# First branches of a two-block transformer kernel: index queries of used tokens only, squares added by GpSimd, rotary swaps as copies, position scores in two products

## The reference, cut to what matters

```python
proj = h @ w_in                                   # c_q 384, c_kv 256, k_pe 64, gate 1024
q = (rms_norm(c_q, q_norm) @ w_uq).reshape(B, L, 8, 192)
q_nope, q_pe = q[..., :128], q[..., 128:]
kv = (rms_norm(c_kv, kv_norm) @ w_ukv).reshape(B, L, 8, 256)
q_pe, k_pe = apply_rope(q_pe, cos, sin), apply_rope(k_pe, cos, sin)   # [x1 cos - x2 sin, x1 sin + x2 cos]
s = q_nope . k_nope + q_pe . k_pe                 # per head; k_pe is shared by the heads
p = softmax(s * 192 ** -0.5);  o = p @ v          # out: (o * silu(gate)) @ w_out
...
# selective attention of the second block, per block of 128 queries
rel = relu(einsum('bqhd,bsd->bqhs', iq, ik) * 64 ** -0.5)
score = einsum('bqh,bqhs->bqs', iw * 8 ** -0.5, rel)      # then causal mask, top 128 of 512 keys
```

## Time and profile before

| | |
|---|---|
| runs | 2126.0 us median of 3 (2125.6 to 2129.88) |
| profiled execution, span | 2125.8 us |
| DVE busy | 1621.4 us, 76% |
| ACT busy | 976.6 us, 46% |
| POOL busy | 399.3 us, 19% |

### The profile page before, as it was taken

The page is one execution under the profiler, slowest core; times in us unless marked ns, Lnnn a source line. Parts: engine busy times, 40 slices in busy tenths (PEclk is TensorE's granted clock), DMA queues, the critical chain, the costliest instruction groups (busy, mean ns, idle before and its releaser), DMA issues.

```text
span 2125.8 us, 29059 instructions
## 1 busy us (share of the span) xinstructions
PE 2098.3 (99%) x10935; PEld 1832.3 (86%) x10935; DVE 1621.4 (76%) x2984; ACT 976.6 (46%) x1710; POOL 399.3 (19%) x296
## 2 busy tenths in 40 slices
PE   8999999999999999999999999999999999999998
PEld 6777788887877788789999999999998888888886
DVE  4777566664985535799999988777668888888887
ACT  5344444444234423533366657766533433333333
POOL 2000110000000001000232323222223344444440
PEclk9999999999999999999999999999999999999999
DMA  6411144531321122123788988898999999999993
GB/s 253 161 38 54 46 148 173 184 130 69 109 92 57 40 99 99 63 97 117 263 281 278 328 285 302 295 311 289 347 366 365 374 372 372 376 376 377 375 364 145
DMA packets 137436, 471.50 MB, mean 222 GB/s; under 512 B 10113, under 2 KB 59521, under 8 KB 111569
## 3 DMA queue, kind: packets, MB, share of 16 engines
q1 hardware_dynamic: 50512, 309.39, 39.9%
q0 software_dynamic: 36864, 134.23, 16.3%
q10 hardware_dynamic: 49920, 26.01, 4.2%
HBM read 417.04 MB, written 52.43 MB: 221 GB/s over the span
## 4 chain that ended last, share of the span: by engine, by line
PE 86%; DVE 10%; DMA 1%; issue 1%; ACT 1%; SPq 0%; DVEq 0%; ACTq 0%
PE bank L156 84%; DVE whl L309 2%; DMA L<-in_w_ada 1%; PE bank L668 1%; DVE L L1480 1%; DVE L L1478 1%; DVE room L2191 1%; DVE L L948 0%; DVE room L2187 0%; PE bank L1569 0%; DVE wk L1914 0%; DMA XT<-in_xT 0%; DVE L L573 0%; DVE L L1461 0%; DVE row L2247 0%
## 5 line engine op out<-in xcount | busy, mean ns | idle before, releaser
L156 PE MATMUL bank<-xhl,whl 128*128 128x384 f32 (+1 forms) x5256 | 1076.2, 361 | 12.2 <-DVE whl L519 7.9
L156 PEld LDWEIGHTS bank<-xhl,whl 128*128 128x128 f32 x5256 | 935.8, 188 | 102.4 <-ACT xhl L459 9.0
L309 DVE TENSOR_TENSOR whl<-raw,whl 128x1024 fp32r<-128x1024 f32 (+2 forms) x389 | 467.4, 1210 | 215.5 <-ACT whl L302 176.9
L156 PE MATMUL bank<-whl,ag 128*128 128x512 f32 x2304 | 526.3, 390 | 0.7 <-issue 0.7
L156 PEld LDWEIGHTS bank<-whl,ag 128*128 128x128 f32 x2304 | 431.4, 188 | 91.3 <-ACT whl L302 1.9
L302 ACT ACTIVATE whl<-raw 128x1024 fp32r<-128x1024 f32 (+2 forms) x389 | 394.3, 1032 | 86.1 <-PE bank L156 78.1
L2234 POOL DMA_INDIRECT row<-in_U_rows,row_at x128 | 177.1, 1384 | 599.2 <-DVE row L2247 431.6
L2234 POOL DMA_INDIRECT row<-in_V_rows,row_at x128 | 180.8, 1413 | 260.2 <-DVE y_tok L2263 231.0
L2263 DVE SCALAR_TENSOR_TENSOR y_tok<-row,row_a,y_tok 128x1024 f32<-128x1024 f32 x127 | 162.4, 1279 | 2.6
L2247 DVE SCALAR_TENSOR_TENSOR row<-row,h_tok 128x1024 f32<-128x1024 f32 x128 | 155.6, 1217 | 1.1 <-DMA row<-in_U_rows,row_at 1.1
L156 PE MATMUL bank<-yhl,whl 128*128 128x512 f32 x588 | 140.2, 395 | 2.7 <-DVE whl L309 2.7
(11 more groups left out here) (278 smaller groups left out, 1977.6 us busy)
## 6 DMA issues: line engine op xcount, KB each, us to landing
raw<-in_U SPq DMA_DIRECT2D x64, 1024.0 KB, 6.8
raw<-in_V SPq DMA_DIRECT2D x64, 1024.0 KB, 7.4
hidden<-h_both SPq DMA_DIRECT2D x32, 768.0 KB, 9.8
gates<-g_stage ACTq DMA_DIRECT2D x12, 2048.0 KB, 19.7
g_ring<-gates SPq DMA_DIRECT2D x32, 768.0 KB, 10.8
h_ring<-hidden SPq DMA_DIRECT2D x22, 768.0 KB, 8.4
raw<-in_w_ada SPq DMA_DIRECT2D x16, 1024.0 KB, 6.4
raw<-in_w_gla SPq DMA_DIRECT2D x12, 1024.0 KB, 4.9
```

Source lines behind the costliest of these rows:

```text
L156: return e.matmul(o, a, b, start=start, stop=stop, skip_group_check=True)
L309: e.tensor_tensor(lo[:, s], src[:, s], F(hi[:, s]), ALU.subtract).then_inc(dve_lo.of((i, half)))
```

## The change

- **Index queries** (`tensor_sel`, `scalar_sel`): only tokens 128 to 511 are projected and copied, 384 columns instead of 512.
- **Squares**: ACT's squares of the latents go to buffers of their own, GpSimd adds those of `c_q` and those of `c_kv` (three `tensor_tensor`), and PE does two `square_sums` after chunk 9 instead of five. Roots and reciprocals (ACT, DVE) move from chunk 9 to chunk 10.
- **Rotary swaps**: `swapped` copies 32 rows at a time from PSUM to the rows of the other half, four copies by ACT, in place of a matmul with `swap`, in `tensor_l0` and for each even head. ACT's copy of `qp` waits in addition until `og` of two heads before is done, since the swapped rows go to `rtmp`.
- **Position scores**: `KD` holds the high part of the keys on rows 0 to 63 and the low part on rows 64 to 127. `QD[j]` holds head j's high queries on both halves (four 64-row copies by ACT for a pair of heads), `q_low` the low parts of both heads (two 64-row subtractions by DVE). A tile takes two matmuls, `QD[j]` with `KD` and `q_low` with `KZ[j]`, instead of three.
- `consts` is laid out without `swap`, and only half of `kz` is zeroed. These lines are left out below.

```diff
         rel, reset = C("rel"), C("reset")
-        rope, swap = cst[:, 384:1408], C("swap")
+        rope = cst[:, 384:1408]
...
         CQ, CK = Parts(yhl, 2560), Parts(yhl, 2560, 3)
-        KZ = Parts(kz, 1024)
+        KZ = [kz[:, j * T:(j + 1) * T] for j in range(2)]
+        KD = kz[:, 2 * T:3 * T]
...
         l0_sq = [l0_tmp[:, 0:T], l0_tmp[:, T:2 * T]]
-        R, l0_dg2, l0_pet = l0_dg, l0_tmp[:, 2 * T:4 * T], l0_sum
+        R, l0_turn, l0_pet = l0_dg, l0_tmp[:, 2 * T:3 * T], l0_sum
+        c_square = [l0_sq[0], l0_sq[1], l0_sq[1], l0_tmp[:, 3 * T:4 * T], l0_sq[1]]
+        c_sum = [c_square[0], c_square[3]]
...
+        def swapped(e, dst, src, done, *step):
...
+            for n in range(4):
+                o = 32 * (n ^ 1)
+                copy(e, dst[32 * n:32 * n + 32], src[o:o + 32]).then_inc(done.of((*step, n)))
...
                 spent[i, ch % 2] = pe_l0, ("in", ch)
-                l0_banks.give(("in", ch), (act_l0, "pe") if ch == 5 else (dve_l0, ("leave", ch)))
+                l0_banks.give(("in", ch), (act_l0, ("swap", 3)) if ch == 5 else (dve_l0, ("leave", ch)))
...
                     l0_banks.give("x root", (act_l0, "R"))
-                for j in (0, 1) if ch == 5 else (ch - 4,) if 6 <= ch < 9 else ():
-                    b = l0_banks.fill(q, "c sum") if j == 0 else l0_banks.of["c sum"]
-                    q.wait_ge(act_l0["c square", j])
-                    square_sums(e, q, b, j // 3, l0_sq[j % 2], j == 0).then_inc(pe_l0.of(("c sum", j)))
-                    if j == 4:
-                        l0_banks.give("c sum", (act_l0, ("c root", 1)))
-                if ch == 6:
-                    b = l0_banks.fill(q, "swap")
-                    q.wait_ge(act_l0["pe"])
-                    mul(e, b, swap, l0_pet, True, True).then_inc(pe_l0.of("swap"))
-                    l0_banks.give("swap", (dve_l0, "swap"))
+                if ch == 9:
+                    b = l0_banks.fill(q, "c sum")
+                    for g in range(2):
+                        q.wait_ge(pool_l0["c sum", 2 + 2 * g])
+                        m = square_sums(e, q, b, g, c_sum[g], g == 0)
+                    m.then_inc(pe_l0.of("c sum"))
+                    l0_banks.give("c sum", (act_l0, ("c root", 1)))
...
                 for j in (0, 1) if ch == 4 else (ch - 3,) if 5 <= ch < 8 else ():
-                    q.wait_ge(dve_l0["leave", j], pe_l0["c sum", j - 2] if j >= 2 else pe_l0["x sum"])
-                    e.activation(l0_sq[j % 2], latent(j), ACT.Square).then_inc(act_l0.of(("c square", j)))
+                    q.wait_ge(dve_l0["leave", j], pe_l0["x sum"])
+                    if j in (2, 4):
+                        q.wait_ge(pool_l0["c sum", 1 if j == 2 else 2])
+                    e.activation(c_square[j], latent(j), ACT.Square).then_inc(act_l0.of(("c square", j)))
...
                     copy(e, l0_pet, l0_banks.of["in", 5]).then_inc(act_l0.of("pe"))
+                    swapped(e, l0_turn, l0_banks.of["in", 5], act_l0, "swap")
                 if ch == 7:
+                    q.wait_ge(dve_l0["kpe"], pool_l0["zeros"])
...
                         rows = slice(64 * n, 64 * n + 64)
-                        q.wait_ge(dve_l0["kpe"], pool_l0["zeros"])
-                        copy(e, KZ(n)[0][rows], kpe[rows]).then_inc(act_l0.of(("kpe", n)))
-                if ch == 9:
-                    q.wait_ge(pe_l0["c sum", 4])
+                        copy(e, KZ[n][rows], kpe[rows]).then_inc(act_l0.of(("kpe", n)))
+                    copy(e, KD[0:64], kpe[0:64]).then_inc(act_l0.of(("kpe", 2)))
+                if ch == 10:
+                    q.wait_ge(pe_l0["c sum"])
...
                 if ch == 6:
-                    q.wait_ge(pe_l0["swap"])
-                    e.tensor_tensor(l0_dg2[:, 0:T], l0_banks.of["swap"], sinT, ALU.mult).then_inc(dve_l0.of("swap"))
+                    q.wait_ge(act_l0["swap", 3])
+                    e.tensor_tensor(l0_turn, l0_turn, sinT, ALU.mult).then_inc(dve_l0.of("swap"))
                     q.wait_ge(dve_l0["swap"])
-                    e.tensor_tensor(kpe, kpe, l0_dg2[:, 0:T], ALU.add).then_inc(dve_l0.of("k turned"))
+                    e.tensor_tensor(kpe, kpe, l0_turn, ALU.add).then_inc(dve_l0.of("k turned"))
...
                 if ch == 7:
-                    for j in range(2):
-                        rows = slice(64 * j, 64 * j + 64)
-                        hi, lo = KZ(j)
-                        q.wait_ge(act_l0["kpe", j], dve_l0["kpe"], pool_l0["zeros"])
-                        e.tensor_tensor(lo[rows], kpe[rows], F(hi[rows]), ALU.subtract).then_inc(dve_l0.of(("kpe", j)))
-                if ch == 9:
+                    q.wait_ge(act_l0["kpe", 1], dve_l0["kpe"])
+                    e.tensor_tensor(KD[64:128], kpe[64:128], F(KZ[1][64:128]), ALU.subtract).then_inc(dve_l0.of("kpe low"))
+                if ch == 10:
...
         def pool_l0_sums(e, q):
-            e.memset(F(kz[:, :]), 0.0).then_inc(pool_l0.of("zeros"))
+            e.memset(F(kz[:, 0:2 * T]), 0.0).then_inc(pool_l0.of("zeros"))
...
                 e.tensor_tensor(l0_sum, l0_sum, l0_sq[(k - 1) % 2], ALU.add).then_inc(pool_l0.of(("sum", k)))
+            for j, g in ((1, 0), (2, 0), (4, 1)):
+                q.wait_ge(act_l0["c square", j])
+                if j == 2:
+                    q.wait_ge(pool_l0["c sum", 1])
+                e.tensor_tensor(c_sum[g], c_sum[g], c_square[j], ALU.add).then_inc(pool_l0.of(("c sum", j)))
...
         loc = Local(L)
-        QN, KN, QP = Parts(yhl, 512, 10), Parts(yhl, 512, 12), Parts(yhl, 512, 14)
+        QN, KN = Parts(yhl, 512, 10), Parts(yhl, 512, 12)
+        QD, q_low = [yhl[:, 14 * T:15 * T], kz[:, 3 * T:4 * T]], yhl[:, 15 * T:16 * T]
...
                     project(e, q, b, iq, 2, CQ, c_ready, 3, 384).then_inc(pe_mla.of(("qp", hd)))
-                    mla_banks.give(("qp", hd), (act_mla, ("qp", hd)))
+                    mla_banks.give(("qp", hd), (act_mla, ("swap", hd, 3)))
...
                 mla_banks.give(("q", hd), (dve_mla, ("q", hd)))
-                if j == 0:
-                    b = mla_banks.fill(q, ("swap", hd))
-                    q.wait_ge(act_mla["qp", hd])
-                    mul(e, b, swap, qraw, True, True).then_inc(pe_mla.of(("swap", hd)))
-                    mla_banks.give(("swap", hd), (dve_mla, ("sin", hd)))
-                else:
+                if j == 1:
...
                 j = hd % 2
-                q.wait_ge(dve_mla["q", hd], dve_mla["k", hd], act_mla["q turned", hd - j], dve_mla["qp", hd - j])
+                q.wait_ge(dve_mla["q", hd], dve_mla["k", hd], act_mla["q turned", hd - j, 3], dve_mla["qp", hd - j, 1])
...
                     mul3(e, b, QN(0, qt * P, (qt + 1) * P), KN(0), True)
-                    mul3(e, b, QP(0, qt * P, (qt + 1) * P), KZ(j), False, True).then_inc(pe_mla.of(("s", hd, qt)))
+                    mul(e, b, QD[j][:, qt * P:(qt + 1) * P], KD, False)
+                    mul(e, b, q_low[:, qt * P:(qt + 1) * P], KZ[j], False, True).then_inc(pe_mla.of(("s", hd, qt)))
...
                     if hd >= 2:
-                        q.wait_ge(pe_mla["swap", hd - 2], dve_mla["cos", hd - 2])
+                        q.wait_ge(dve_mla["cos", hd - 2], act_mla["og", hd - 2], dve_mla["og", hd - 2])
                     copy(e, qraw, mla_banks.of["qp", hd]).then_inc(act_mla.of(("qp", hd)))
+                    swapped(e, rtmp, mla_banks.of["qp", hd], act_mla, "swap", hd)
...
                     q.wait_ge(dve_mla["q turned", hd])
-                    copy(e, QP(0)[0], qp).then_inc(act_mla.of(("q turned", hd)))
+                    for n in range(4):
+                        rows, own = slice(64 * (n % 2), 64 * (n % 2) + 64), slice(64 * (n // 2), 64 * (n // 2) + 64)
+                        copy(e, QD[n // 2][rows], qp[own]).then_inc(act_mla.of(("q turned", hd, n)))
...
                     hi, lo = at(0)
-                    q.wait_ge(act_mla[what, hd], pe_mla[what, hd] if what in "qk" else dve_mla[what, hd])
+                    q.wait_ge(act_mla[what, hd], pe_mla[what, hd])
...
                         q.wait_ge(pe_mla["s", hd - 1, 3])
-                    e.tensor_tensor(lo, whole, F(hi), ALU.subtract).then_inc(dve_mla.of((what if what in "qk" else "qp", hd)))
+                    e.tensor_tensor(lo, whole, F(hi), ALU.subtract).then_inc(dve_mla.of((what, hd)))
...
                     if hd >= 2:
-                        q.wait_ge(act_mla["q turned", hd - 2], dve_mla["qp", hd - 2])
+                        q.wait_ge(act_mla["q turned", hd - 2, 3], dve_mla["qp", hd - 2, 1])
...
                 if hd % 2 == 0:
-                    q.wait_ge(pe_mla["swap", hd])
-                    if hd >= 2:
-                        q.wait_ge(act_mla["og", hd - 2], dve_mla["og", hd - 2])
-                    e.tensor_tensor(rtmp, mla_banks.of["swap", hd], sinT, ALU.mult).then_inc(dve_mla.of(("sin", hd)))
+                    q.wait_ge(act_mla["swap", hd, 3])
```

(31 more changed lines are left out.)

## The result

The changed kernel takes 2128.8 us (median of 20 runs, 2126.86 to 2133.85), the kernel before 2125.94 (20 runs, 2123.52 to 2130.9). The ratio is 1.0014, 95% interval 1.0008 to 1.0021: 2.9 us slower, less than the 4.3 us that the prediction counts as a change. The profiled execution has a span of 2125.4 us and a time of 2127.11. It is the third quickest of the 20, so its span does not show the 2.9 us; its stages show where time is lost and won.

The account below looks back on a forecast made before the run. Bound: the loop of DVE and `w_ada` loads in the first projections, PE in attention and before the index scores. +1.4 + 1.6 + 3.4 - 4.4 = +2.0 on 2125.8, with the median's 0.2, gave 2128.0 us; range 2119 to 2132.5.

Parts of the forecast that it names:

- First projections, saving worth 0: First projection stage: PE's saved square sums and swap, some 3.5 us, shorten nothing, as DVE and `w_ada` loads set the pace.
- The place: First projections, the spread at PE's chunk 11 that needs the reciprocal: PE idles about 3 us there, near 82 to 85.
- GpSimd's sums, +1.4: First projections: three new GpSimd sums delay DVE by 0 to 0.9 us each, taken as 0.45: +1.4 us (0 to 2.7).
- Attention's path, +1.6: Attention, even heads: the longer path through ACT and DVE makes the two-head loop 34.3 us against 33.9: +1.6 us.
- The clock, +3.4: Attention: gaps of 3.1 us before even scores drop PE to 1.2 GHz, 1.7 us per fall: +3.4 us (0 to 6.8).
- Two of four: Attention: of four chances for a clock fall ahead of even heads' scores, two were taken, halfway between two profile rows.
- Index queries, -4.4: Before the index scores: 96 products of 384 instead of 512 columns save 0.046 us each, moving later stages forward: -4.4 us.
- the overlap of copies: Rival, attention: narrow copies overlap, the clock holds, GpSimd finds free moments: -6.6 and the median's 0.2, 2119.4 us; chance 0.20.
- the saving kept by PE: Rival, attention: the new path stays hidden and PE keeps its saving of 10.8 us: -13.8, 2112.2 us; chance 0.08.
- the index stage without effect: Rival, index stage: DVE's selection is the bound, so the change has no effect there: +4.4 on the forecast, 2132.4; chance 0.06.
- No fall at all: Rival, attention: the clock never falls in the gaps before even scores: 3.4 us less, 2124.6; chance 0.18.
- Four falls in every run: Rival, attention: the clock falls before all even heads' scores, 6.8 us in place of 3.4: 2131.4; chance 0.18.

Follow-up runs that it names:

- the filled gaps: The changed kernel with useless products in TensorE's gaps ahead of the even heads' scores (13 in head 0, 9 in heads 2, 4, 6): 2125.01 us.

## Why the prediction was right

The forecast of 2128.0 lies 0.8 us below the measured median. Its terms, each against its runs (index -5.7, first projections +3.5, attention +4.9, in sum +2.7 of the 2.9 measured; each is the difference of one run to the next in a chain, so the sum is no check of them). The mechanisms held, but part of the closeness is luck: the index queries gained 1.3 us more than forecast by medians, the first projections cost 2.1 more, and the two errors largely cancel (0.4 and 1.0 by means).

- **First projections, saving worth 0:** held. The place was right in part: in four of the seven profiles with GpSimd's sums PE idles 1.1 to 1.5 us at the spread, never 3. In the changed kernel the saving is used up sooner, in waits of 0.96, 1.43 and 0.17 us from 58 to 74 us that DVE's late splits cause, and a fall of the clock behind them (0.82 in the first window above, 0.75 in the next); at the spread in the changed kernel there is no gap left.
- **GpSimd's sums, +1.4:** the mechanism held and the profiles agree in size, 0.8 to 1.3. The working behind it did not. They cost DVE 2.4 us, not half of 2.7: all three met a DVE instruction, two of them for most of a sum's length. That delay passes on in full to the next load of the loop. By the means of the same 13 profiles the load of `w_ada` near 76 us is issued 2.4 us later, and 1.0 comes back because it then lands sooner, 4.6 to 5.1 us after its issue in all seven profiles with the sums, against 6.0 to 6.7 in four of the six without and 4.7 in the other two. Why the load took longer in those four no run shows; that the net cost lies near the forecast is luck. By median times the stage costs 3.5, by means 2.4 with an interval down to 0.8, so this term may be too small; what the rest is made of no run shows.
- **Attention's path, +1.6:** held. The loop was put at 34.3 us and is 34.4; the gaps at 3.1 and are 2.15 to 3.73; narrow copies are held, at 0.61 and 0.65 us where 0.63 and 0.66 were taken. With the falls taken out, attention costs 4.9 - 3.8 = 1.1 by medians (1.4 by means).
- **The clock, +3.4:** held; 3.8 by the filled gaps. Two of four was a guess between two rows: 3.8 at 1.7 each is 2.2 falls, an average over runs, while the profile of the changed kernel shows one fall of four and that with the squares on TensorE two.
- **Index queries, -4.4:** right in mechanism, short by 0.8 against the trace. The price of a 384-column product was taken from the expert stage, 0.1835 us; here it is 0.177, against 0.232 for 512 columns, and 96 x 0.055 = 5.3, 5.2 in the trace.

Of the rivals, the overlap of copies fell by the trace (0.61 apart), the saving kept by PE fell by the gaps, and the index stage without effect fell by the run of that part alone. No fall at all (2124.6) is what the filled gaps show: 2125.0. Four falls in every run (2131.4) would be more than the changed kernel's median; only three of its 20 runs reach that time.

The change as a whole is two gains and two losses. The gain that its attention part promised (7.4 us of scores) was there for the taking: the swap copies, one of its parts, lengthened the path through ACT that the shorter scores were now waiting for. With the swap left on TensorE the kernel takes 2116.5 us, 0.5% under the kernel before.

## What to carry to other kernels

Work moved off the busiest engine must be walked as a path, not weighed as a sum: 0.86 us of TensorE in every second head became 2.5 us of ScalarE copies ahead of its scores, and with the wait the saving of another edit was lost too. A wait of 2 to 4 us on TensorE can have two prices, its length and half of the time at the lower clock behind it, if the clock falls; filling it with idle products tells them apart in one run. And where a stage is paced by loads that the loop itself issues, follow a delay to the next load's issue and then to its landing: here 2.4 us arrived in full at the issue and 1.0 came back only because that load was quicker, so the net cost was known no better than the load's own spread.

## What the runs showed of the hardware

- A gap does not always bring the clock down. Of the gaps of 2.1 us or more ahead of attention's first products and scores, in all profiles, 3.73, 3.74, 3.14, 2.88 (twice), 2.30 and 2.10 us were followed by windows under 1.00, and 2.90, 2.89, 2.58, 2.16, 2.15 and 2.14 us were not. So the length alone does not decide, and what does no run shows. None of the gaps of 1.93 us or less there was followed by such a window; in the first projections, on the other hand, the clock fell near 72 us behind gaps of 1.5 us and less in three of the seven profiles with GpSimd's sums.
- ScalarE lets copies overlap on equal rows even if their heights differ (0.47 to 0.48 us apart, from PSUM), and holds them when the rows change (0.61 from PSUM, 0.65 from SBUF).
- An f32 `scalar_tensor_tensor` of DVE with both inputs in SBUF is held by GpSimd's `tensor_tensor` (2.30 us instead of 1.22, beside a sum of 1.43), and the sum in turn if DVE is first: the third started 0.24 us after a DVE product, took 2.12 and ended 1.1 us after that product did. The Trainium skill (SBUF — State Buffer, section SBUF: two separate sides) states this as a lock that whichever starts first holds for its whole instruction, also between a VectorE instruction with two SBUF inputs and a GpSimd one that reads SBUF; these rows agree.
- Two executions of the same first projections, up to 100 us, end 1.9 us apart (last split at 98.58 and 96.72), as the `w_ada` load near 80 us is waited for 4.81 or 3.38 us (kernel before, and the run of the index queries alone). An effect of 1 us there is not to be read from one profile.
